# GpSimd makes the lower half of every second weight block of the up stage, from the eighth on

## The chip, the cores and the metric

One core of one Trainium2 chip runs the whole kernel. The metric is device time in microseconds (us). The engines have separate queues and meet only at semaphores: TensorE (PE) multiplies matrices, VectorE (DVE), ScalarE (ACT) and GpSimd (POOL) work elementwise, SyncE (SP) issues DMAs, and GpSimd issues the indirect ones (gathers of rows).

## What is computed

A decoder layer on 512 tokens of width 1024: a mixer, a cross-attention and a PEER channel mixer. Only the last matters here. Each token picks 16 of 16384 one-neuron experts for each of 8 heads and sums what they give:

```
u = jnp.take(expert_down, idx, axis=0)
a = jax.nn.gelu(jnp.einsum('nd,nhkd->nhk', xb, u).astype(jnp.float32), approximate=False)
w = (gb * a).astype(xb.dtype)
v = jnp.take(expert_up, idx, axis=0)
return jnp.einsum('nhk,nhkd->nd', w, v)
```

## The kernel before, in words

For three of the four tiles of 128 tokens (less 32 tokens) the kernel computes all experts densely: the down stage multiplies the activations with 128 blocks of 128 experts, and the **up stage** multiplies the gated result with the 128 blocks of `up_in` (128x1024 each, 512 KB). The fourth tile, the sparse one, gathers its rows of `up_in` one choice after the other: 128 gathers, each of which brings one row for each of the 128 tokens, and 128 weighted additions to `x`.

Float32 products are made of halves: a number is split into a rounded high part and a low part (the rest), and `three` adds high by high, high by low and low by high. So the up stage needs for every block `up_high` and `up_low` of the weights, and `wgt_high` and `wgt_low` of the gated activations.

The work on block u in the up stage, by engine:

- SP loads the block into one of eight places (`uraw`), when the product of block u-8 is done, and the gates and activations besides.
- ACT writes `up_high` (`high_up`, L585), as soon as the product of block u-4 is done, since there are four places for it; then `wgt_high` (L589).
- DVE goes through turns, one for each block (the loop at L1388 for blocks 0 to 14, the one at L1399 from 15 on). Turn u: `low_up(u)` makes `up_low` of block u (L1353, in the place of `uraw`), `weigh(u+1)` multiplies gates and activations of the next block (L1371, L1375), `weight_low(u)` makes `wgt_low` (L1382), and `sparse_up(u-1)` adds one gathered row to the sparse tile (L1361).
- POOL issues the 128 gathers in order (the loop at L528, L539). There are eight places for them; gather k waits for the addition of gather k-8 (`sparse_added`). Gathers 0 to 7 wait besides for the end of the down stage and for the first products, since their places are used before by other things.
- PE waits for `up_low` and `w_ready` of the block and then does 18 matmuls (`second_product`, L1776).

The order on each engine is written out by hand; no scheduler changes it. In the profile, `kept` and `arena` are the large buffers in which most of the named tensors lie.

Of the kernel before, what the change touches and what calls it, by code (L numbers as in the profile page):

```python
# [5 lines left out]
F32 = mybir.dt.float32  # L6
# [3 lines left out]
ALU = mybir.AluOpType  # L10
# [18 lines left out]
NK = 128  # L29
# [28 lines left out]
SLOTS = PH * TK  # L58
RING_A, RING_B, RING_C = 7, 4, 8
RING_U = 8  # L60
EDGE = 32
PARTS = P // EDGE
EDGE_SLOTS = SLOTS // PARTS
DE = DN - EDGE
E0, E_BASE = P - EDGE, P - 32
ROWS = SLOTS + EDGE_SLOTS
# [36 lines left out]
def build(nc, x_in, mem_in, vecs_in, final_in, ffn_in, front_w, keys_in, down_in, down_rows, up_in, out, gate_dram, hid_dram):  # L103
    ctx = ExitStack()
    with ctx:
        def sem(name):
            return ctx.enter_context(nc.semaphore(name))
# [4 lines left out]
        with ExitStack() as over:  # L112
            def aliased(name, kb, shape, now):
                if kb > now:
                    over.enter_context(nc.sbuf_tensor(f"pad{kb}", [P, (kb - now) * KB], F32))
                return over.enter_context(nc.sbuf_tensor(name, [P] + shape, F32R))
# [5 lines left out]
            up_hi = aliased("up_high", 140, [4, D], 133)  # L122
            memT_half = [aliased("memT_high", 188, [KC, NM], 156), aliased("memT_low", 196, [KC, NM], 196)]
            w_half = (w_hi, w_low)
        with ExitStack() as over:
            up_lo = aliased("up_low", 76, [RING_U, D], 0)
        with ExitStack() as over:
# [14 lines left out]
        def at(kb, n, *dims):  # L142

            where, kb = (kept, kb) if kb < 44 else (under_w, kb - 44) if kb < 60 else (arena, kb - 60)
            a = where[:, int(kb * KB):int(kb * KB) + n]
            if len(dims) == 2:
                return a.rearrange("p (a b) -> p a b", a=dims[0])
            if len(dims) == 3:
                return a.rearrange("p (a b c) -> p a b c", a=dims[0], b=dims[1])
            return a  # L150
# [91 lines left out]

        uraw = at(76, RING_U * D, RING_U, D)
        wraw = at(108, 4 * DN, 4, DN)
# [12 lines left out]
        ld_b = [sem(f"ld_down_rows_b{j}") for j in range(RING_B)]  # L257
        ld_c = [sem(f"ld_up_rows{j}") for j in range(RING_C)]
        dot_done, gel3_ready, sparse_added = sem("dot_done"), sem("gel3_ready"), sem("sparse_added")
        up_high, up_low = sem("up_high"), sem("up_low")  # L260
        consts = sem("consts")

        class Norm:
# [35 lines left out]
        stored = [sem(f"gates_stored{s}") for s in range(2)]  # L299
        ld_up = [sem(f"ld_up{s}") for s in range(RING_U)]  # L300
        ld_gate = [sem(f"ld_gate{s}") for s in range(4)]
# [27 lines left out]
        def up_slot(u):  # L329
            return (u + RING_U // 2) % RING_U  # L330

# [7 lines left out]
        def _(sp):  # L339
# [26 lines left out]
            def load_up(i, s):  # L366
                sp.dma_start(uraw[:, up_slot(s), :], up_in[bass.ds(i, 1)].rearrange("b p n -> (b p) n")).then_inc(ld_up[s], 16)

            def load_gates(i, s):

                sp.dma_start(gates[s], gate_dram[:, :, bass.ds(i * CH, GT * CH)]).then_inc(ld_gate[s], 16)
# [4 lines left out]
            def block_of(u):  # L376
                return u + SPILL if u < KEEP else u - KEEP
# [18 lines left out]
            load_gates(block_of(GT), 1)  # L396
            for u in range(5, RING_U):
                load_up(block_of(u), u)
            load_gates(block_of(2 * GT), 2)

            for s in range(2):
                sp.wait_ge(hid_stored[s], 16 * (SPILL // 2))
            for u in range(RING_U, KEEP):
                sp.wait_ge(up_done, u + 1 - RING_U)
# [34 lines left out]
        def _(pool):  # L439
# [57 lines left out]
            k = 0  # L497
# [27 lines left out]
            assert k == ROWS  # L525

            up_rows = up_in.rearrange("b p n -> (b p) n")
            for k in range(SLOTS):  # L528
                if k < RING:
                    pool.wait_ge(block_used, USED + NK - RING + k + 1)  # L530
                elif k == RING:
                    pool.wait_ge(block_used, USED + NK)
                if RING <= k < RING_C:
                    pool.wait_ge(up_done, k - RING + 1)
                if RING + 2 <= k < RING_C:
                    pool.wait_ge(w_raw, 2 * (3 if k == RING + 2 else 6))
                if k >= RING_C:
                    pool.wait_ge(sparse_added, k - RING_C + 1)
                nc.gpsimd.indirect_dma_start(rows_c[k % RING_C], None, up_rows,  # L539
                                             bass.IndirectOffsetOnAxis(idx3[:, k:k + 1].bitcast(U32), 0))\  # L540
                    .then_inc(ld_c[k % RING_C], 16)

        @block.scalar
        def _(act):
# [282 lines left out]
            def early_at(i):  # L827
                early(i, i % 4, 16 * ((USED + i + 2) // 4 + 1), USED + i + 1, 16 * (i // 2) if i > 1 else None, i + 3, i == 0)
# [9 lines left out]
            for q in range(PARTS):  # L838
                early_at(4 + q)
                act.dma_start(edge_h[q * EDGE:(q + 1) * EDGE], hn[E0:P, DT - 1, :].rearrange("p (k n) -> p k n", k=KC))\  # L840
                    .then_inc(edge_moved, 16)
# [9 lines left out]
            for n in range(DT):  # L851
# [3 lines left out]
                if n == 0:  # L855
                    early_at(EXP_AT[0])
                    for q in range(PARTS):
                        if q < 3:
                            early_at(EXP_AT[0] + 1 + q)
                        if q == 0:  # L860
                            act.wait_ge(idx_ready, 2)
                        act.dma_start(edge_idx[q * EDGE:(q + 1) * EDGE, :],
                                      idx_last[E0:P, q * EDGE_SLOTS:(q + 1) * EDGE_SLOTS]).then_inc(edge_moved, 16)
# [17 lines left out]
            for n in range(STEPS):  # L881
# [6 lines left out]
                if GEL_AT <= n < GEL_AT + PARTS:  # L888
                    q = n - GEL_AT
                    act.dma_start(edge_back[E0:P, q * EDGE_SLOTS:(q + 1) * EDGE_SLOTS],  # L890
                                  edge_gel[q * EDGE:(q + 1) * EDGE, :]).then_inc(edge_moved, 16)
                if n == LAST_TURN:
# [72 lines left out]
        def _(dve):  # L965
# [382 lines left out]
                nc.vector.memset(ones_of[:, :, DE:DN], 1.0).then_inc(edge_ones, 1)  # L1348


            def low_up(i, s):
                dve.wait_ge(up_high, i + 1)
                nc.vector.tensor_tensor(up_lo[:, up_slot(s), :], uraw[:, up_slot(s), :], up_hi[:, s % 4, :].bitcast(F32),  # L1353
                                        ALU.subtract).then_inc(up_low, 1)
# [9 lines left out]
            def weigh(i, s, quad, gate_landed, landed, block, kept_hid=None):  # L1364
                dve.wait_ge(ld_gate[quad], gate_landed)
                if kept_hid is None:
                    dve.wait_ge(ld_hid[s % 4], landed)
                else:
                    dve.wait_ge(gelu_out, landed)
                h = hidr[:, s % 4, :] if kept_hid is None else kept_hid  # L1370
                nc.vector.tensor_tensor(  # L1371
                    wraw[:, s % 4, 0:FAR * CH].rearrange("p (c n) -> p c n", n=CH),
                    h[:, 0:FAR * CH].rearrange("p (c n) -> p c n", n=CH),
                    gates[quad][:, :, (s % 4) * CH:(s % 4 + 1) * CH], ALU.mult).then_inc(w_raw, 1)
                nc.vector.tensor_tensor(  # L1375
                    wraw[:, s % 4, FAR * CH:].rearrange("p (i n) -> p i n", i=1),
                    h[:, FAR * CH:].rearrange("p (i n) -> p i n", i=1),
                    stage[:, FAR % 2, bass.ds(block, 1), :], ALU.mult).then_inc(w_raw, 1)

            def weight_low(i, s):  # L1380
                dve.wait_ge(w_high, i + 1)
                nc.vector.tensor_tensor(wgt_half[1][:, s, :], wraw[:, s, :], wgt_half[0][:, s, :].bitcast(F32),  # L1382
                                        ALU.subtract).then_inc(w_ready, 1)
# [2 lines left out]
            dve.wait_ge(edge_ones, len(hid_ones))  # L1386
            weigh(0, 0, 0, 16, SPILL + 3, SPILL, hid_kept[0])
            for s in range(15):  # L1388
                low_up(s, s % RING_U)
                weigh(s + 1, s + 1, (s + 1) // 4, 16, SPILL + s + 4, SPILL + s + 1, hid_kept[s + 1])  # L1390
                weight_low(s, s % 4)
                if s == 0:
                    dve.wait_ge(gel3_ready, 1)
                    step(nc.vector.tensor_tensor(w3, gel3, gate3, ALU.mult))
                else:
                    sparse_up(s - 1, (s - 1) % 8, 16 * ((s - 1) // 8 + 1), s - 1 if s > 1 else None)
# [40 lines left out]
        def _(pe):  # L1437
# [333 lines left out]
            def up_operands(o, s):  # L1771
                d = slice((o % 2) * 512, (o % 2 + 1) * 512)
                return ([w[:, s % 4, (o // 2) * P:(o // 2 + 1) * P] for w in wgt_half],
                        [up_hi[:, s % 4, d], up_lo[:, up_slot(s), d]])

            def second_product(i, s, first=False):  # L1776

                pe.wait_ge(up_low, i + 1)
                pe.wait_ge(w_ready, i + 1)
                for o in range(2 * DT):  # L1780
                    if first and o in (4, 5):
                        pe.wait_ge(gelu_out, NK + o - 3)
                    ins = three(psum[:, o, :], *up_operands(o, s), first, False)
                ins.then_inc(up_done, 1)
# [43 lines left out]
                second_product(s, s)  # L1828
            with pe.Fori(1, NK // RING_U - 1) as r:
                for s in range(RING_U):  # L1830
                    second_product(r * RING_U + s, s)
            for s in range(RING_U - 2):
                second_product(NK - RING_U + s, s)
            pe.wait_ge(up_low, NK)
            pe.wait_ge(w_ready, NK)
            for o in range(2 * DT):
                for s in (RING_U - 2, RING_U - 1):
# [50 lines left out]
```

## Time and profile before

| what | us |
|---|---|
| median of 3 runs | 1627.9 (1626.72 to 1633.07) |
| the profiled execution | 1624.01 |
| its span, first to last instruction | 1622.3 |
| up stage in it, first to last `up_low` subtraction | 1085.0 to 1600.7 |

All numbers of the trace are of this one execution, in us from the start of its span; the time outside the span is 1.7 us. A timeline row gives start, duration, engine, line, operation, output<-inputs with shapes, and in brackets how long the engine had been idle before it and what ended that. An instruction's duration overlaps with the next one's start by about 0.1 on DVE.

### The profile page before, as it was taken

What the parts mean: (1) busy time and instruction counts of PE and PEld (TensorE: products, weight loads), DVE (VectorE), ACT (ScalarE), POOL (GpSimd) and SP (SyncE); (2) the same over time, 40 slices, a digit from 0 to 9 for tenths busy, and PEclk for the clock granted to TensorE, in tenths of its full rate; (3) what the DMA queues carried; (4) which work ended last, traced back from release to release, by engine and by line L of the source; (5) the groups of instructions that cost most, each with busy time, mean ns of one, the idle gap of its engine ahead of it and who ended that gap; (6) DMA issues with size and microseconds to landing.
All of it is one profiled execution on the core that took longest, in us unless ns stands there. A gap on an engine that the chain in (4) does not pass through costs nothing.

```text
span 1622.3 us, 26556 instructions
## 1 busy us (share of the span) xinstructions
PE 1600.3 (99%) x9227; PEld 1422.6 (88%) x9227; DVE 1133.7 (70%) x2214; ACT 673.2 (41%) x998; POOL 829.1 (51%) x523
## 2 busy tenths in 40 slices
PE   8999999999999999999999999999999999999998
PEld 6888888788889999999999999998888888888886
DVE  4155451351509999996999898329888888888887
ACT  5342453451534343534545544444333333333333
POOL 4463276423244998987787777866422222222220
PEclk9999999999999999999999999999999999999999
DMA  4322242313434999997999999949999999999992
GB/s 184 93 100 71 75 151 94 104 53 117 146 102 131 347 340 332 329 335 233 339 405 394 387 403 401 362 158 391 400 348 350 331 349 339 349 334 348 339 331 77
DMA packets 154425, 424.69 MB, mean 262 GB/s; under 512 B 15728, under 2 KB 65904, under 8 KB 154224
## 3 DMA queue, kind: packets, MB, share of 16 engines
q1 hardware_dynamic: 89088, 229.41, 40.5%
q0 software_dynamic: 41472, 151.01, 25.5%
q10 hardware_dynamic: 23792, 43.33, 6.9%
q8 instruction: 42, 0.69, 0.2%
q14 instruction: 31, 0.25, 0.0%
HBM read 379.88 MB, written 43.25 MB: 261 GB/s over the span
## 4 chain that ended last, share of the span: by engine, by line
PE 69%; issue 16%; POOL 9%; DVE 2%; DMA 2%; ACT 1%; POOLq 0%; SPq 0%; ACTq 0%; DVEq 0%
PE psum L1471 22%; PE psum L1473 22%; PE psum L1472 22%; POOL w_low L461 8%; PE psum L1766 4%; DMA gate_dram<-arena 1%; DMA kept<-down_in 1%; POOL arena L493 1%; DMA arena<-down_rows,arena 0%; DVE arena L1258 0%; ACT w_high L581 0%; DVE arena L1202 0%; DVE arena L1193 0%; DVE arena L1194 0%; DMA kept<-front_w 0%
## 5 line engine op out<-in xcount | busy, mean ns | idle before, releaser
L461 POOL TENSOR_TENSOR w_low<-kept,w_high 128x1024 fp32r<-128x1024 f32 x212 | 519.5, 2454 | 320.3 <-ACT w_high L581 317.6
L1471 PE MATMUL psum<-hT_high,w_high 128*128 128x352 f32 (+2 forms) x1408 | 484.4, 344 | 7.2 <-POOL w_low L461 5.5
L1473 PE MATMUL psum<-hT_high,w_low 128*128 128x352 f32 (+2 forms) x1408 | 476.6, 339 | 0.0
L1472 PE MATMUL psum<-hT_low,w_high 128*128 128x352 f32 (+2 forms) x1408 | 476.4, 338 | 0.0
L581 ACT ACTIVATE w_high<-kept 128x1024 fp32r<-128x1024 f32 x212 | 224.0, 1058 | 202.6 <-DMA kept<-down_in 102.0
L1471 PE MATMUL psum<-up_high,wgt_high 128*128 128x512 f32 x768 | 298.8, 389 | 0.0
L1473 PE MATMUL psum<-up_high,wgt_low 128*128 128x512 f32 x768 | 298.8, 389 | 0.0
L1472 PE MATMUL psum<-up_low,wgt_high 128*128 128x512 f32 x768 | 298.8, 389 | 0.0
L1471 PEld LDWEIGHTS psum<-hT_high,w_high 128*128 128x128 f32 x1408 | 264.8, 188 | 24.2 <-POOL w_low L461 8.2
L1473 PEld LDWEIGHTS psum<-hT_high,w_low 128*128 128x128 f32 x1408 | 264.7, 188 | 12.7
L1472 PEld LDWEIGHTS psum<-hT_low,w_high 128*128 128x128 f32 x1408 | 264.8, 188 | 12.3 <-issue 0.5
L585 ACT ACTIVATE up_high<-arena 128x1024 fp32r<-128x1024 f32 x128 | 135.8, 1061 | 309.0 <-PE psum L1473 307.2
L1182 DVE CUSTOM_DVE_ANT_0 arena<-arena,psum 128x1024 f32<-128x1024 f32 x160 | 191.1, 1215 | 45.4 <-DMA arena<-down_rows,kept 42.6
L1353 DVE TENSOR_TENSOR up_low<-arena,up_high 128x1024 fp32r<-128x1024 f32 x128 | 156.9, 1226 | 76.4 <-ACT up_high L585 76.4
L1472 PEld LDWEIGHTS psum<-up_low,wgt_high 128*128 128x128 f32 x768 | 144.2, 188 | 29.9
L1471 PEld LDWEIGHTS psum<-up_high,wgt_high 128*128 128x128 f32 x768 | 144.2, 188 | 29.9
L1473 PEld LDWEIGHTS psum<-up_high,wgt_low 128*128 128x128 f32 x768 | 144.2, 188 | 29.8
L539 POOL DMA_INDIRECT arena<-up_in,kept x64 | 70.8, 1106 | 179.1 <-DVE kept L1361 166.4
L539 POOL DMA_INDIRECT kept<-up_in,kept x64 | 71.5, 1118 | 165.9 <-DVE kept L1361 157.7
L493 POOL DMA_INDIRECT arena<-down_rows,kept x128 | 121.8, 951 | 62.1 <-DVE kept L1182 30.4
L822 ACT ACTIVATE arena<-psum 128x352 f32<-128x352 f32 x112 | 51.9, 464 | 114.3 <-PE psum L1473 92.1
L1325 DVE TENSOR_TENSOR arena<-arena,psum 128x3072 bf16<-128x3072 bf16 x48 | 83.9, 1748 | 0.0
(252 smaller groups left out, 1956.4 us busy)
## 6 DMA issues: line engine op xcount, KB each, us to landing
kept<-down_in SPq DMA_DIRECT2D x128, 512.0 KB
arena<-up_in SPq DMA_DIRECT2D x128, 512.0 KB, 4.7
kept<-front_w SPq DMA_DIRECT2D x92, 512.0 KB
gate_dram<-arena ACTq DMA_DIRECT2D x40, 512.0 KB
hid_dram<-arena ACTq DMA_DIRECT2D x112, 176.0 KB
arena<-hid_dram SPq DMA_DIRECT2D x112, 176.0 KB
under_w<-gate_dram SPq DMA_DIRECT2D x24, 640.0 KB
arena<-gate_dram SPq DMA_DIRECT2D x8, 640.0 KB
```

The lines of the kernel that those rows point to most:

```text
L461: nc.gpsimd.tensor_tensor(w_low[:, s, :], ring[:, s, :], w_hi[:, s, :].bitcast(F32), ALU.subtract).then_inc(low_ready, 1)
L493: nc.gpsimd.indirect_dma_start(ring[slot], None, down_rows, bass.IndirectOffsetOnAxis((edge_idx if edge else idx3)[:, j:j + 1].bitcast(U32 ...
L539: nc.gpsimd.indirect_dma_start(rows_c[k % RING_C], None, up_rows, bass.IndirectOffsetOnAxis(idx3[:, k:k + 1].bitcast(U32), 0))\
L581: nc.scalar.activation(w_hi[:, s, :], ring[:, s, :], ACT.Copy).then_inc(high_ready, 1)
L585: nc.scalar.activation(up_hi[:, s % 4, :], uraw[:, up_slot(s), :], ACT.Copy).then_inc(up_high, 1)
L1182: nc.vector.tensor_tensor_reduce(ring[slot], ring[slot], h_row, 1.0, 0.0, ALU.mult, ALU.add, (edge_dot if edge else dot3)[:, j:j + 1]).the ...
L1325: nc.vector.tensor_tensor(hot_g[:, s], hot_i.rearrange("p (n q) i r -> p n q i r", q=1).to_broadcast(each), pieces[:, m:m + PAIRS].rearran ...
L1353: nc.vector.tensor_tensor(up_lo[:, up_slot(s), :], uraw[:, up_slot(s), :], up_hi[:, s % 4, :].bitcast(F32), ALU.subtract).then_inc(up_low, 1)
L1471: nc.tensor.matmul(out, lhs[0], rhs[0], start=first, stop=False)
L1472: nc.tensor.matmul(out, lhs[0], rhs[1], start=False, stop=False)
L1473: return nc.tensor.matmul(out, lhs[1], rhs[0], start=False, stop=last)
L1766: ins = nc.tensor.matmul(psum[:, (2 * h + m) % 3, t % 4 * P:(t % 4 + 1) * P], hot_j[:, h % HOTS, t // 2, :, t % 2], hot_g[:, h % HOTS, t / ...
```

## The change

From block 8 on, POOL makes `up_low` of the even blocks (60 of them, 8 to 126), DVE makes those of the odd blocks and of blocks 0 to 7. POOL does the subtraction of block u right behind its gather u+5, and the last two (124 and 126) behind gather 127. It signals on a semaphore of its own, `even_up_low`, on which PE waits for even blocks from 8 on. Nothing else is changed.

```diff
+POOL_UP = 8
...
+            def even_low_up(u):
+                s = u % RING_U
+                pool.wait_ge(up_high, u + 1)
+                nc.gpsimd.tensor_tensor(up_lo[:, up_slot(s), :], uraw[:, up_slot(s), :], up_hi[:, s % 4, :].bitcast(F32),
+                                        ALU.subtract).then_inc(even_up_low, 1)
+
             for k in range(SLOTS):
...
                 nc.gpsimd.indirect_dma_start(rows_c[k % RING_C], None, up_rows,
                                              bass.IndirectOffsetOnAxis(idx3[:, k:k + 1].bitcast(U32), 0))\
                     .then_inc(ld_c[k % RING_C], 16)
+                if k % 2 and k >= POOL_UP + 5:
+                    even_low_up(k - 5)
+            for u in range(SLOTS - 4, NK, 2):
+                even_low_up(u)
...
-            def low_up(i, s):
+            def low_up(i, s, late=True):
+                if late and s % 2 == 0:
+                    return
...
-                low_up(s, s % RING_U)
+                low_up(s, s % RING_U, s >= POOL_UP)
...
-            def second_product(i, s, first=False):
-
-                pe.wait_ge(up_low, i + 1)
+            def second_product(i, s, first=False, pairs=None):
+
+                if pairs is None:
+                    pe.wait_ge(up_low, i + 1)
+                elif s % 2:
+                    pe.wait_ge(up_low, pairs + (POOL_UP // 2 + (s + 1) // 2))
+                else:
+                    pe.wait_ge(even_up_low, pairs + (s // 2 + 1 - POOL_UP // 2))
```

POOL's queue at the start of the up stage, before. The first row is the last ten subtractions of the down stage, the others are the gathers 0 to 15, four to a row (by the buffer that they write):

```order
L461 TENSOR_TENSOR w_low<-kept,w_high 128x1024 x10
L539 DMA kept<-up_in,kept 128x1024 x4
L539 DMA arena<-up_in,kept 128x1024 x4
L539 DMA kept<-up_in,kept 128x1024 x4
L539 DMA arena<-up_in,kept 128x1024 x4
```

And with the change, up to gather 17:

```order
L462 TENSOR_TENSOR w_low<-kept,w_high 128x1024 x10
L546 DMA kept<-up_in,kept 128x1024 x4
L546 DMA arena<-up_in,kept 128x1024 x4
L546 DMA kept<-up_in,kept 128x1024 x4
L546 DMA arena<-up_in,kept 128x1024 x2
L532 TENSOR_TENSOR up_low<-arena,up_high 128x1024
L546 DMA arena<-up_in,kept 128x1024 x2
L532 TENSOR_TENSOR up_low<-arena,up_high 128x1024
L546 DMA kept<-up_in,kept 128x1024 x2
```

The subtraction of block 8 stands behind gathers 12 and 13, that of block 10 behind 14 and 15.

DVE's queue in turns 7 and 8, before, and the start of turn 9:

```order
L1353 TENSOR_TENSOR up_low<-arena,up_high 128x1024
L1371 TENSOR_TENSOR arena<-arena,under_w 128x320
L1375 TENSOR_TENSOR arena<-arena 128x64
L1382 TENSOR_TENSOR wgt_low<-arena,wgt_high 128x384
L1361 SCALAR_TENSOR_TENSOR kept<-arena,kept 128x1024
L1353 TENSOR_TENSOR up_low<-arena,up_high 128x1024
L1371 TENSOR_TENSOR arena<-arena,under_w 128x320
L1375 TENSOR_TENSOR arena<-arena 128x64
L1382 TENSOR_TENSOR wgt_low<-arena,wgt_high 128x384
L1361 SCALAR_TENSOR_TENSOR kept<-arena,kept 128x1024
L1353 TENSOR_TENSOR up_low<-arena,up_high 128x1024
```

And with the change (the lines are 13 further down):

```order
L1366 TENSOR_TENSOR up_low<-arena,up_high 128x1024
L1384 TENSOR_TENSOR arena<-arena,under_w 128x320
L1388 TENSOR_TENSOR arena<-arena 128x64
L1395 TENSOR_TENSOR wgt_low<-arena,wgt_high 128x384
L1374 SCALAR_TENSOR_TENSOR kept<-arena,kept 128x1024
L1384 TENSOR_TENSOR arena<-arena,under_w 128x320
L1388 TENSOR_TENSOR arena<-arena 128x64
L1395 TENSOR_TENSOR wgt_low<-arena,wgt_high 128x384
L1374 SCALAR_TENSOR_TENSOR kept<-arena,kept 128x1024
L1366 TENSOR_TENSOR up_low<-arena,up_high 128x1024
```

The subtraction has left turn 8; the other four instructions of the turn are the same.

## Rows read from the trace of the kernel before

**Rows 1.** The page, part 1: TensorE over the whole span.
```profile
PE 1600.3 (99%) x9227; PEld 1422.6 (88%) x9227; DVE 1133.7 (70%) x2214; ACT 673.2 (41%) x998; POOL 829.1 (51%) x523
```

**Rows 2.** Busy time in the up stage: PE, PEld, DVE, ACT, POOL, clock, DMA.
```profile
1093.00:1610.00 517.00, 517.00 (x2283) 428.32 (x2282) 435.56 (x634) 189.56 (x258) 139.53 (x126) 1.00 0.93 334
```

**Rows 3.** Waits from 1095 to 1602: engine, line, releaser, total, times, longest.
```profile
ACT up_high L585 <- PE psum L1473: 307.2, 120, 2.7
DVE up_low L1353 <- ACT up_high L585: 74.8, 115, 0.7
```

**Rows 4.** Timeline of one steady turn on ACT, DVE and POOL.
```profile
1154.87 1.06 ACT L585 ACTIVATE up_high<-arena 128x1024 fp32r<-128x1024 f32 x1 [2.61 <-PE psum L1473]
1155.96 1.23 DVE L1353 TENSOR_TENSOR up_low<-arena,up_high 128x1024 fp32r<-128x1024 f32 x1 [0.65 <-ACT up_high L585]
1157.64 0.55 DVE L1382 TENSOR_TENSOR wgt_low<-arena,wgt_high 128x384 fp32r<-128x384 f32 x1
1158.11 1.28 DVE L1361 SCALAR_TENSOR_TENSOR kept<-kept 128x1024 f32<-128x1024 f32 x1
1160.04 1.23 DVE L1353 TENSOR_TENSOR up_low<-arena,up_high 128x1024 fp32r<-128x1024 f32 x1 [0.65 <-ACT up_high L585]
...
1159.66 0.94 POOL L539 DMA_INDIRECT kept<-up_in,kept  x1 [3.14 <-DVE kept L1361]
```

**Rows 5.** Timeline of POOL in the down stage: subtraction, gather, subtraction.
```profile
899.14 2.40 POOL L461 TENSOR_TENSOR w_low<-kept,w_high 128x1024 fp32r<-128x1024 f32 x1 [0.81 <-ACT w_high L581]
901.69 0.95 POOL L493 DMA_INDIRECT arena<-down_rows,kept  x1
902.70 2.39 POOL L461 TENSOR_TENSOR w_low<-kept,w_high 128x1024 fp32r<-128x1024 f32 x1
```

**Rows 6.** Timelines: two places where POOL subtracts beside DVE.
```profile
104.75 3.63 POOL L461 TENSOR_TENSOR w_low<-kept,w_high 128x1024 fp32r<-128x1024 f32 x1 [7.20 <-ACT w_high L581]
...
106.04 2.39 DVE L1023 COPY kept<-arena 128x32 f32<-128x32 f32 x1
...
1086.62 2.82 POOL L461 TENSOR_TENSOR w_low<-kept,w_high 128x1024 fp32r<-128x1024 f32 x1 [4.55 <-ACT w_high L581]
...
1087.12 2.47 DVE L1394 TENSOR_TENSOR kept<-kept 128x128 f32<-128x128 f32 x1
```

**Rows 7.** Timeline of POOL: gathers 6, 8, 9, 10 and 13.
```profile
1106.14 1.88 POOL L539 DMA_INDIRECT arena<-up_in,kept  x1 [3.14 <-PE psum L1473]
...
1111.67 3.03 POOL L539 DMA_INDIRECT kept<-up_in,kept  x1 [0.30 <-issue]
1115.01 3.03 POOL L539 DMA_INDIRECT kept<-up_in,kept  x1 [0.30 <-issue]
1118.35 3.03 POOL L539 DMA_INDIRECT kept<-up_in,kept  x1 [0.30 <-issue]
...
1128.36 3.03 POOL L539 DMA_INDIRECT arena<-up_in,kept  x1 [0.30 <-issue]
```

**Rows 8.** Timeline of DVE: turn 5 in part, then turn 8 and the next start.
```profile
1106.12 0.49 DVE L1371 TENSOR_TENSOR arena<-arena,under_w 128x320 f32<-128x320 f32 x1
...
1118.34 1.23 DVE L1353 TENSOR_TENSOR up_low<-arena,up_high 128x1024 fp32r<-128x1024 f32 x1
1119.47 0.49 DVE L1371 TENSOR_TENSOR arena<-arena,under_w 128x320 f32<-128x320 f32 x1
1120.01 0.56 DVE L1382 TENSOR_TENSOR wgt_low<-arena,wgt_high 128x384 fp32r<-128x384 f32 x1
1120.47 1.29 DVE L1361 SCALAR_TENSOR_TENSOR kept<-arena,kept 128x1024 f32<-128x1024 f32 x1
1121.67 1.23 DVE L1353 TENSOR_TENSOR up_low<-arena,up_high 128x1024 fp32r<-128x1024 f32 x1
```

**Rows 9.** Timelines of PE and ACT where block 8's product begins.
```profile
1126.11 0.39 PE L1471 MATMUL psum<-up_high,wgt_high 128*128 128x512 f32 x1
...
1126.31 1.06 ACT L585 ACTIVATE up_high<-arena 128x1024 fp32r<-128x1024 f32 x1 [2.31 <-PE psum L1473]
```

More of the change, by code:

```diff
@@ L259, in build @@
         dot_done, gel3_ready, sparse_added = sem("dot_done"), sem("gel3_ready"), sem("sparse_added")
-        up_high, up_low = sem("up_high"), sem("up_low")
+        up_high, up_low, even_up_low = sem("up_high"), sem("up_low"), sem("even_up_low")
         consts = sem("consts")
@@ L1830, in _ @@
                 for s in range(RING_U):
-                    second_product(r * RING_U + s, s)
+                    second_product(r * RING_U + s, s, pairs=r * (RING_U // 2))
             for s in range(RING_U - 2):
-                second_product(NK - RING_U + s, s)
-            pe.wait_ge(up_low, NK)
+                second_product(NK - RING_U + s, s, pairs=(NK - RING_U) // 2)
+            pe.wait_ge(up_low, (NK + POOL_UP) // 2)
+            pe.wait_ge(even_up_low, (NK - POOL_UP) // 2)
             pe.wait_ge(w_ready, NK)
```

## The prediction

> **What bounds the kernel now.** I read the page first: TensorE is busy for 1600.3 of 1622.3 us [rows 1]. Then the busy time by stretches: in the up stage from 1093 to 1610 PE is busy for all of its 517 us, VectorE (DVE) for 435.6 and GpSimd (POOL) for 139.5 [rows 2]. The list of waits in the stage has no row in which PE waits at all; the longest is ScalarE (ACT), which waits 307.2 us for PE, and DVE waits 74.8 us for ACT, 115 times at most 0.7 [rows 3]. So PE sets the pace and the others follow it. One steady turn shows the distances [rows 4]: a turn is 1160.04 - 1155.96 = 4.08 us. ACT writes the high half of block u at 1154.87, when PE has ended block u-4; PE wants block u three turns later, at 1154.87 + 3 x 4.08 = 1167.1, and DVE has its last half ready at 1157.64 + 0.55 = 1158.2, 8.9 us early. A faster DVE can therefore give nothing here. The question is only whether POOL is ever late.
>
> **What goes.** 60 subtractions leave DVE, each 1.13 us from its start to that of the next instruction (1118.34 to 1119.47) [rows 8]. All of it lay beside PE: worth 0 on the path. What PE itself gets, one semaphore for another, I set at 0.
>
> **What comes, in the steady part.** POOL's subtraction of the same shape in the down stage takes 2.40 us, 0.06 behind a gather (901.69 + 0.95 to 902.70), and the next gather comes 0.15 behind it [rows 5]. It does not run freely beside DVE. A DVE instruction of 128x128 that met one took 2.47 us and a copy of 128x32 took 2.39 us [rows 6]: they stood until POOL was through. And POOL's own took 3.63 us where it met a long DVE instruction. They exclude each other, one whole instruction at a time. The Trainium skill says so (SBUF — State Buffer, "Who interferes with whom"): a DVE instruction with two SBUF inputs and a GpSimd instruction that reads SBUF take one shared read interface in turns, and the later one blocks fully; by that rule, too, every DVE instruction of a turn is exposed, and these rows agree.
>
> So DVE's load for two blocks is: a full turn back to back, 1121.67 - 1118.34 = 3.33; a turn without the subtraction, 3.33 - 1.13 = 2.20 [rows 8]; and up to 2.40 of standing still: 7.93 us, of 2 x 4.08 = 8.16. It still fits, by 0.23 us. Its place in the turn is kind: POOL may begin when ACT has written the high half, at 1154.87 + 1.06 = 1155.9, and is done at 1158.4; DVE's `wgt_low` then ends at 1158.9, where PE wants it at 1167.1. That leaves 8.2 us of cover. POOL's own load is 2.40 + 0.06 + 0.15 + two gathers of 0.94 with 0.30 between, 4.8 of 8.16 us, if the gathers stay at 0.94 [rows 4]. Queued behind the waiting subtraction are only the next gathers, with eight places, so that DVE wants a gather some seven turns after it can be issued. Cost of the steady part: 0.
>
> **What comes, at block 8.** Here the trace speaks against the change. The first subtraction is queued behind gather 13, and POOL is behind at that time: gather 8 starts at 1111.67, and it and the six behind it follow each other at 0.30 us with 3.03 us each, gather 13 from 1128.36 to 1131.39 [rows 7]. PE starts block 8 at 1126.11 [rows 9]. What it waits for would not even have been begun. A gather alone takes 0.94; it takes 3.03 where it begins with DVE's subtraction (1118.35 and 1118.34) and DVE then runs without a gap, and 1.88 where it begins with the next instruction (gather 6 at 1106.14, DVE's L1371 at 1106.12) [rows 7, 8]. Both ends lie 0.8 behind the end of DVE's L1382 (1120.01 + 0.56 = 1120.57, and the gather's 1121.38). The Trainium skill gives another rule (SBUF — State Buffer, the same section): a `tensor_tensor` is inferred not to hold up descriptor generation. By it the gathers would be short; the rows of 3.03 us beside nothing but such instructions say otherwise, and I go by the rows. What the rule would make of block 8 is the second rival.
>
> With the change DVE's turns 8 and 10 are short, so I lay the two queues side by side:
>
> - DVE: turn 8 starts at 1118.34 and takes 2.20, to 1120.54; turn 9 takes 3.33, to 1123.87; turn 10 takes 2.20, to 1126.07. Turn 11 has to wait for its high half, which ACT writes from 1126.31 to 1127.37 [rows 9]. So DVE is idle from about 1126.1 to 1127.4.
> - POOL: gather 10 at 1118.35 now begins with L1371: 1.88, to 1120.23. Gather 11 at 1120.53 begins with DVE's subtraction 9: 3.03, to 1123.56. Gather 12 at 1123.86 begins with L1371: 1.88, to 1125.74. Gather 13 at 1126.04 finds DVE idle: 0.94, to 1126.98. The subtraction of block 8 starts at 1127.04, ahead of DVE's at 1127.4, and takes 2.40, to 1129.44.
>
> PE could start at 1126.11 and starts at about 1129.5: **3.4 us of standstill**, which nothing gives back, since PE is full from there to the end. Bounds: at least 0, if the gathers 10 to 13 are 0.94 each (1118.35 + 4 x 1.24 + 2.40 = 1125.7, just in time); at most, gather 13 as before to 1131.39 and 2.46 more: 1133.85, which is 7.7 us, and up to 2.3 more if DVE's row of instructions is ahead of POOL at the port. I take 3.4, since its terms are the nearest rows.
>
> **Block 10 and on.** From 1129.5 every deadline is 3.4 us later: block 10 at 1129.5 + 8.16 = 1137.7. POOL has gathers 14 and 15 before it. From 1129.6, with DVE in a full turn 11, they take 1.9 to 3.0 and 0.94 to 1.9, then 0.6 of gaps and 2.40: done between 1135.4 and 1137.5. Just in time, with 0.2 to 2.3 us to spare; from then on POOL needs less than 8.16 for a pair and gains. Cost 0, upper bound about 2.
>
> **The sum.** 0 (DVE) + 0 (steady) + 3.4 (block 8) + 0 (block 10). The profiled execution of 1624.0 would become 1627.4; it lies 3.9 below the median, and the step is the same on it: 1627.9 + 3.4 = **1631.3 us**.
>
> **The rivals.**
>
> 1. *The gathers stay long, or block 10 stalls as well.* Gathers 8 to 14 are all 3.03 now, whatever else DVE does; for it: seven equal rows. Against: gather 6 with 1.88 and the idle gap that turn 11 gets. It gives 6 to 9 us: 1634 to 1637.
> 2. *POOL is in time.* If gathers 10 to 13 are 0.94 each, the standstill is 0, and the change is not seen at all: 1627.9. For it: the steady gather has 0.94 [rows 4]. Against: DVE has gaps in those turns, and not at block 8 until 1126.1.
> 3. *Slower by much: the pair does not fit.* A mechanism of the whole stage: with DVE at 7.93 of 8.16 us it has hardly gaps left, and the gathers may go back to 3.03 all along. Then POOL's pair is 2 x 3.03 + 0.30 + 0.06 + 0.15 + 2.40 = 8.97 us. It decides from 8.16 + 8.2 / 60 = 8.30 us on, where the cover is used up over the 60 pairs. At 8.97 the price is 60 x 0.81 - 8.2 = 40 us, or 1668; but each standstill of PE gives DVE gaps and shortens the gathers, so I expect 8.4 to 8.7 in this case: 6 to 24 us, 1637 to 1655. For it: the seven rows, just where DVE has no gap. Against: every pair has one turn in which DVE waits for ACT's high half, and one of the two gathers can fall there.
> 4. *It does not do what it says.* The queues show that DVE sheds one subtraction in two and POOL has it. Excluded, but for a side effect that I don't see.
>
> **How the numbers follow.** My forecast (2 to 5 us slower) 0.46; rival 1, 0.22; rival 2, 0.13; rival 3, 0.15; anything else, a gain among it, 0.04. About 0.5%, 8.1 us, is what a measurement of this kernel can tell from no change; so slower by more means over 1636.0: rival 3 and a fifth of rival 1, 0.19. A gain needs a PE wait that is not there: 0.02. The same: 0.79. The range goes from 1627 (rival 2, with the runs' lower half) to 1642, through rival 1 and the cheaper third of rival 3; above it lies about 0.1, below about 0.06.
>
> **What the changed profile would show.** Right: one wait of PE's first matmul of block 8 on POOL's `up_low`, 3 to 4 us, and no other wait of PE from there to 1610; POOL's first subtraction starting near 1127; gathers 10 and 12 below 2 us; steady POOL subtractions at 2.4 and a DVE instruction beside each with about 2 us more than before; DVE waiting for `up_high` once in two turns or less. Wrong: no PE wait (the gathers are not held up), a wait of 7 us and more (they are not shortened), or many PE waits spread to the end, with POOL never idle (rival 3).

## The result, and the profile after

| | median, us | before, measured beside it | ratio to before, 95% interval |
|---|---|---|---|
| changed | 1637.84 (1634.48 to 1639.96, 7 runs) | 1627.9 (1625.83 to 1633.36, 7 runs) | 1.0054 (1.0036 to 1.0073) |
| changed, measured again | 1636.0 (1631.24 to 1641.46, 6 runs) | 1627.18 (17 runs) | 1.0058 (1.0037 to 1.0078) |
| changed, a third time | 1632.73 (1628.02 to 1641.15, 10 runs) | 1627.02 (16 runs) | 1.0036 (1.002 to 1.0053) |

The change makes the kernel slower, by 6 to 10 us from median to median. The forecast was 3.4 slower, the range to 1642. The profiled execution took 1639.96 us, its span is 1638.2. Its line of the page that answers to [rows 1], and the two new or changed groups (line, engine, operation, count | busy us, mean ns | idle before, releaser):

```profile
PE 1605.0 (98%) x9227; PEld 1424.5 (87%) x9227; DVE 1173.1 (72%) x2154; ACT 671.6 (41%) x998; POOL 1016.0 (62%) x583
...
L532 POOL TENSOR_TENSOR up_low<-arena,up_high 128x1024 fp32r<-128x1024 f32 x60 | 144.2, 2404 | 128.8 <-ACT up_high L596 128.7
L1395 DVE TENSOR_TENSOR wgt_low<-arena,wgt_high 128x384 fp32r<-128x384 f32 x128 | 180.4, 1409 | 42.0 <-ACT wgt_high L600 42.0
```

POOL has 187 us more, as 60 subtractions at 2.4 us (144.2) and longer gathers make it: from 1150 to 1600 a gather takes 1.41 us in the mean (154.9 us for 110), where before it took 0.94. DVE did 60 instructions less and was yet *busier*, by 39 us: its L1395 (L1382 before, 0.55 us each [rows 4]) now has a mean of 1.41, since it stands still behind POOL.

The waits from 1085 to the end (who waited for whom: us in total, times, longest), where before PE had no row at all:

```profile
DVE wgt_low L1395 <- ACT wgt_high L600: 42.0, 58, 11.2
...
PE psum L1484 <- POOL up_low L532: 7.7, 1, 7.7
...
DVE arena L1384 <- DMA under_w<-gate_dram: 6.4, 1, 6.4
...
PE psum L1484 <- DVE wgt_low L1395: 1.6, 1, 1.6
```

There is one wait of PE on POOL's `up_low`, of 7.7 us, at block 8. The wait for `wgt_low` ends at 1110.7, before block 8, in turns that the change does not touch. The list has one more wait of PE, 0.4 us for the last subtraction of the down stage. Busy time by stretches (PE, PEld, DVE, ACT, POOL, granted clock, DMA share, GB/s), to be held against [rows 2]:

```profile
1093.00:1130.00 37.00, 35.44 (x163) 29.68 (x163) 28.66 (x44) 15.23 (x21) 21.49 (x12) 1.00 0.95 346
1130.00:1150.00 20.00, 12.32 (x42) 9.55 (x41) 8.85 (x13) 2.94 (x4) 16.82 (x10) 0.74 0.84 303
1150.00:1600.00 450.00, 450.00 (x1987) 372.60 (x1986) 418.80 (x498) 162.88 (x221) 286.48 (x165) 1.00 0.96 341
```

Apart from the 1.6 us ahead of 1130, all is lost in the 20 us around block 8; from 1150 to 1600 PE is busy all the time. And the middle row has a clock of 0.74. The place itself, POOL first (gathers 10, 11, 12, 13, then block 8's subtraction; compare [rows 7]), then DVE's subtraction of turn 11, then PE:

```profile
1125.00 1.90 POOL L546 DMA_INDIRECT kept<-up_in,kept  x1 [0.30 <-issue]
1127.21 3.03 POOL L546 DMA_INDIRECT kept<-up_in,kept  x1 [0.30 <-issue]
1130.55 1.90 POOL L546 DMA_INDIRECT arena<-up_in,kept  x1 [0.30 <-issue]
1132.75 3.03 POOL L546 DMA_INDIRECT arena<-up_in,kept  x1 [0.30 <-issue]
1135.80 3.10 POOL L532 TENSOR_TENSOR up_low<-arena,up_high 128x1024 fp32r<-128x1024 f32 x1
...
1132.74 1.22 DVE L1366 TENSOR_TENSOR up_low<-arena,up_high 128x1024 fp32r<-128x1024 f32 x1
...
1130.98 0.39 PE L1486 MATMUL psum<-up_high,wgt_low 128*128 128x512 f32 x1
1139.04 0.79 PE L1484 MATMUL psum<-up_high,wgt_high 128*128 128x512 f32 x1 [7.67 <-POOL up_low L532]
1139.63 0.63 PE L1485 MATMUL psum<-up_low,wgt_high 128*128 128x512 f32 x1
1140.05 0.63 PE L1486 MATMUL psum<-up_high,wgt_low 128*128 128x512 f32 x1
...
1145.45 0.39 PE L1484 MATMUL psum<-up_high,wgt_high 128*128 128x512 f32 x1
```

Gathers 10 to 12 took 1.90, 3.03, 1.90, as laid out. Gather 13 took 3.03. DVE was later, against PE, than in the trace of before: it had no gap at turn 11, and its subtraction started 0.01 us ahead of the gather. Then PE: its first matmul comes at 1139.04 where 1131.21 was due, 7.8 late. And the next ones follow at 0.42 to 0.43 us, not 0.23 [rows 9 has the place before]: 15 steps in 6.41 us, where 15 x 0.227 = 3.4 were due. The granted clock there is 0.50:

```profile
1139.00:1145.00 6.00, 5.96 (x14) 4.71 (x15) 0.00 (x0) 0.00 (x0) 5.22 (x4) 0.50 0.60 204
```

That is the lower of the two clock levels (1.2 GHz) behind a pause, and 3.0 us more.

Of the 15.9 us between the two profiled executions, 10.8 are this. The rest lies ahead of the first instruction that the change moves: the gates landed 3.3 us later for the first turn (1087.68 against 1084.41), and 1.6 are the wait for `wgt_low` ahead of block 8. That neither is an effect of the change is inferred from their place and not tested by itself.

### The profile page after: what moved, and what is told of

Same layout as the page of the kernel before. It is cut to its first block, busy times and chain, and to the rows that moved or that the text cites. A ratio compares the mean times of both kernels' runs of the same rounds, so it can differ in the third digit from the quotient of the medians.

```text
span 1638.2 us, 26542 instructions
## 1 busy us (share of the span) xinstructions
PE 1605.0 (98%) x9227; PEld 1424.5 (87%) x9227; DVE 1173.1 (72%) x2154; ACT 671.6 (41%) x998; POOL 1016.0 (62%) x583
## 4 chain that ended last, share of the span: by engine, by line
PE 62%; issue 16%; POOL 11%; DMA 5%; DVE 4%; ACT 1%; POOLq 0%; SPq 0%; DVEq 0%; ACTq 0%
PE psum L1484 20%; PE psum L1486 19%; PE psum L1485 19%; POOL w_low L462 9%; PE psum L1779 3%; DMA kept<-down_in 2%; POOL arena L494 1%; DMA under_w<-gate_dram 1%; DVE arena L1336 1%; DVE arena L1193 1%; DMA arena<-down_rows,kept 1%; POOL kept L546 1%; ACT w_high L592 1%; POOL arena L546 0%; DMA arena<-gate_dram 0%
## 5 line engine op out<-in xcount | busy, mean ns | idle before, releaser
L532 POOL TENSOR_TENSOR up_low<-arena,up_high 128x1024 fp32r<-128x1024 f32 x60 | 144.2, 2404 | 128.8 <-ACT up_high L596 128.7
L1395 DVE TENSOR_TENSOR wgt_low<-arena,wgt_high 128x384 fp32r<-128x384 f32 x128 | 180.4, 1409 | 42.0 <-ACT wgt_high L600 42.0
L546 POOL DMA_INDIRECT arena<-up_in,kept x64 | 90.8, 1418 | 36.9 <-DVE kept L1374 18.2
L546 POOL DMA_INDIRECT kept<-up_in,kept x64 | 94.7, 1480 | 27.0 <-DVE kept L1374 16.0
```

Source lines behind the costliest of these rows:

```text
L532: nc.gpsimd.tensor_tensor(up_lo[:, up_slot(s), :], uraw[:, up_slot(s), :], up_hi[:, s % 4, :].bitcast(F32), ALU.subtract).then_inc(even_up ...
```

## The experiments

**1. The change again, beside the others.** It was measured twice more, each time beside other kernels.

> The change once more, beside the three variants on the same chip. Theory (a standstill of TensorE at block 8 and a fall of its clock behind it): 8 to 12 us over the kernel before, one wait of 6 to 8 us on GpSimd's first subtraction, granted clock below 1 in the stretch behind it, no other wait on GpSimd. Rival (the steady load of the shared port costs as well): the same total, but with small waits spread to the end.

> The change once more, as the partner of the two others on the same chip: 7 to 11 us over the kernel before; a wait of TensorE of about 4.2 us where GpSimd's gather 13 takes 0.94 us, of about 7.7 us where it takes 3.03.

The medians were 1636.0 and 1632.73 us. The wait on POOL was 4.2 us in the first trace and 3.3 in the second, with no other wait on POOL's subtraction. The second trace, POOL's gathers 10 to 13 and the subtraction, and PE:

```profile
1120.30 1.90 POOL L546 DMA_INDIRECT kept<-up_in,kept  x1 [0.30 <-issue]
1122.50 3.03 POOL L546 DMA_INDIRECT kept<-up_in,kept  x1 [0.30 <-issue]
1125.84 1.89 POOL L546 DMA_INDIRECT arena<-up_in,kept  x1 [0.31 <-issue]
1128.04 0.94 POOL L546 DMA_INDIRECT arena<-up_in,kept  x1 [0.30 <-issue]
1129.00 2.36 POOL L532 TENSOR_TENSOR up_low<-arena,up_high 128x1024 fp32r<-128x1024 f32 x1
...
1131.49 0.79 PE L1484 MATMUL psum<-up_high,wgt_high 128*128 128x512 f32 x1 [3.33 <-POOL up_low L532]
1132.08 0.63 PE L1485 MATMUL psum<-up_low,wgt_high 128*128 128x512 f32 x1
...
1134.98 0.39 PE L1486 MATMUL psum<-up_high,wgt_low 128*128 128x512 f32 x1
```

This is the prediction's picture: 1.88, 3.03, 1.88, 0.94, then 2.40, and a wait of 3.4. Block 8 was due at 1128.0 and began 3.5 us late. Behind that come 1.7 us of slow matmuls (1131.49 to 1134.98 is 8 steps: 3.49, less 8 x 0.227), so 5.2 in all; in the first of the two traces it is 4.4 and 1.7, 6.1 in all. What differs between the executions is how long DVE waited for the first gates from DRAM (`under_w`) in turn 3. In the three traces of the change it waited 3.1, 4.0 and 6.4 us, and PE 3.3, 4.2 and 7.7. The two kernels of experiment 7, which have the same order on POOL, fit in: 3.2 and 5.4 us for the gates, and 3.4 and 5.0 from the time that PE was due at block 8 to the end of the subtraction.

The last step, from 5.0 to 7.7, is gather 13, and it hangs on very little. Here it is in the kernel with eight fillers of experiment 7, with DVE's subtraction of turn 11:

```profile
1131.19 0.94 POOL L546 DMA_INDIRECT arena<-up_in,kept  x1 [0.31 <-issue]
...
1131.21 1.23 DVE L1366 TENSOR_TENSOR up_low<-arena,up_high 128x1024 fp32r<-128x1024 f32 x1
```

DVE has no gap here either, but the gather began 0.02 us ahead of the subtraction, and took 0.94; in the profiled execution it began 0.01 behind it, and took 3.03.

The change's runs spread over 13 us (1628 to 1641) and those of before over 6 to 8. The wait for the gates would explain that, but runs without a trace cannot show it; what they do show is a lower granted clock in the slowest (0.996 at 1637.5 and 1641.2 us, 0.998 or 0.999 at 1628.0 and 1630.2).

**2. From block 16 on.**

```diff
-POOL_UP = 8
+POOL_UP = 16
...
-            for s in range(1, RING_U):
-                second_product(s, s)
-            with pe.Fori(1, NK // RING_U - 1) as r:
+            for s in range(1, POOL_UP):
+                second_product(s, s % RING_U)
+            with pe.Fori(POOL_UP // RING_U, NK // RING_U - 1) as r:
```

> GpSimd takes the even blocks from 16 on instead of from 8 on, 56 subtractions instead of 60; all else as in the change. Theory (all of the loss is the place of the first subtraction in GpSimd's queue, when it is behind): by block 16 the gathers have caught up, so no wait of TensorE on GpSimd; 0 us, within 0.15% of the kernel before; VectorE's instructions beside the subtractions still take about 2 us more. Rival (the exclusion of the two engines costs): 56 of 60 parts of the loss stay, 8 to 10 us slower than before.

1626.61 us, ratio 0.9999 (0.999 to 1.0008). PE has no wait on POOL, and its stretch is full again; DVE still stands beside each subtraction:

```profile
1093.00:1610.00 517.00, 517.00 (x2290) 428.96 (x2289) 478.67 (x580) 190.13 (x258) 329.74 (x185) 1.00 0.93 334
...
1299.83 2.44 DVE L1395 TENSOR_TENSOR wgt_low<-arena,wgt_high 128x384 fp32r<-128x384 f32 x1 [0.53 <-ACT wgt_high L600]
```

So 56 of the 60 subtractions cost nothing that these runs can tell (the interval ends 1.3 us above the kernel before). The loss needs a subtraction among the first four, at the place that they have in the queue.

**3. Earlier in the queue.**

```diff
-                if k % 2 and k >= POOL_UP + 5:
+                if k in (9, 11, 13, 15):
+                    even_low_up(k - 1)
+                if k % 2 and k >= 21:
                     even_low_up(k - 5)
```

> The same 60 subtractions as the change, from block 8 on, but those of blocks 8, 10, 12 and 14 stand behind gathers 9, 11, 13 and 15 (the change: 13, 15, 17 and 19), and the one of block 16 behind gather 21 as in the change. Theory (place in the queue): GpSimd's first subtraction starts near 1118 to 1122 in place of 1136, TensorE does not wait, 0 us against the kernel before, at most 0.15%. Rival (GpSimd or the port has too much to do at this time, wherever the subtraction stands): TensorE waits 3 us or more at block 8, 10 or 12, or the gathers come late and VectorE waits for them; 5 us or more slower.

1632.79 us, ratio 1.0036 (1.0022 to 1.0051): the expected 0 was missed, by 5.6 us. Block 8 and the next three have no wait. But block 16, which keeps its place behind gather 21, has one. POOL from block 14's subtraction to block 16's (the six gathers between take 1.3 to 3.0 us), and PE's wait:

```profile
1143.40 4.47 POOL L532 TENSOR_TENSOR up_low<-arena,up_high 128x1024 fp32r<-128x1024 f32 x1 [1.32 <-ACT up_high L598]
1148.03 1.76 POOL L546 DMA_INDIRECT kept<-up_in,kept  x1
...
1160.40 1.90 POOL L546 DMA_INDIRECT arena<-up_in,kept  x1 [0.30 <-issue]
1162.32 2.58 POOL L532 TENSOR_TENSOR up_low<-arena,up_high 128x1024 fp32r<-128x1024 f32 x1
...
1165.03 0.62 PE L1486 MATMUL psum<-up_high,wgt_high 128*128 128x512 f32 x1 [2.82 <-POOL up_low L532]
```

The standstill moved to the next subtraction that has six gathers ahead of it. DVE, stopped by the early subtractions, had no gap (it was busy for all 20 us from 1130 to 1150), and the gathers were long. Block 16 began 3.0 us late, and the slow matmuls behind the pause cost 1.7 more. I had not seen that when I chose block 16's place: the mistake of the change, made once more at another block.

**4. Fewer gathers ahead, throughout.** All 60 subtractions, the one of block u behind gather u+1 (lead 1, the edit below), or behind gather u+3 (lead 3).

```diff
-                if k % 2 and k >= POOL_UP + 5:
-                    even_low_up(k - 5)
-            for u in range(SLOTS - 4, NK, 2):
-                even_low_up(u)
+                if k % 2 and k >= POOL_UP + 1:
+                    even_low_up(k - 1)
```

> The same 60 subtractions; the one of block u stands behind gather u+1 throughout (the change: u+5). Theory: the first one starts near 1120 to 1123, there is never a row of several gathers ahead of one (as ahead of block 16 in the second variant), and TensorE does not wait: 0 us, within 0.15% of the kernel before. Rival (the next gathers now stand behind a subtraction that waits for ScalarE, and come too late): VectorE waits for gathers in every pair, and if that exceeds 8 us of cover TensorE waits for wgt_low; 5 us or more slower.

> The same 60 subtractions; the one of block u stands behind gather u+3. Theory (the wait grows with the number of gathers ahead): the first one starts behind gather 11, near 1130, and ends at 1132.5 to 1133.5, where TensorE wants it near 1130 to 1132: a wait of 0.5 to 2.5 us and about 1 us of slow matmuls, 1 to 3 us slower than before (ratio 1.0005 to 1.002), between the variant with lead 1 and the change. Rival (it depends on how busy the port is, not on the place): the same wait as in the change, 4 to 8 us.

Lead 1: 1627.34 us, ratio 0.9999 (0.999 to 1.0009). Lead 3: 1629.77, ratio 1.0024 (1.0009 to 1.0039), a bit more than the 1.002 expected. The first subtraction with lead 1, and with lead 3 together with PE's place:

```profile
1121.94 3.62 POOL L532 TENSOR_TENSOR up_low<-arena,up_high 128x1024 fp32r<-128x1024 f32 x1
```

```profile
1126.97 3.60 POOL L532 TENSOR_TENSOR up_low<-arena,up_high 128x1024 fp32r<-128x1024 f32 x1
...
1128.94 0.39 PE L1486 MATMUL psum<-up_high,wgt_low 128*128 128x512 f32 x1
1130.71 0.49 PE L1484 MATMUL psum<-up_high,wgt_high 128*128 128x512 f32 x1 [1.39 <-POOL up_low L532]
1131.04 0.40 PE L1485 MATMUL psum<-up_low,wgt_high 128*128 128x512 f32 x1
1131.28 0.39 PE L1486 MATMUL psum<-up_high,wgt_low 128*128 128x512 f32 x1
```

Lead 1, 3, 5: no wait, 1.4 us, 3.3 to 7.7 us. The same work, only its place is different. Note that the pause of 1.4 us leaves the clock alone: the matmuls behind it are back at 0.23. The traced execution of lead 3 (1628.7 us) lost 1.6 us at block 8; its 12 runs reach up to 1637.22. Where those lost more is not shown.

**5. The wait alone.** VectorE makes everything as before; TensorE only waits until GpSimd has come past gather 13.

```diff
                     .then_inc(ld_c[k % RING_C], 16)
+                if k == 13:
+                    nc.gpsimd.memset(at(23.25, 1), 0.0).then_inc(passed, 1)
...
             for s in range(1, RING_U):
                 second_product(s, s)
+            pe.wait_ge(passed, 1)
```

In its first form it had `pool.sem_inc(passed, 1)` in place of the memset:

> The kernel before, VectorE makes all lower halves; the only edit is that TensorE, ahead of block 8, also waits until GpSimd has issued gather 13, the place at which the change's first subtraction stands. Theory (the place in the queue does it, not the subtraction): the gathers 8 to 13 all take 3.03 us since VectorE has no gap, gather 13 ends some 5 us after TensorE wants block 8, and the clock falls behind it: 5 to 8 us slower (ratio 1.003 to 1.005). Rival (the subtraction itself or its contention makes the loss): a wait below 2 us, the time of the kernel before.

1627.11 us, ratio 1.0002 (0.9989 to 1.0015), and no wait of PE, though gather 13 ended at 1133.75 and PE started block 8 near 1128.5. The increment was not ordered behind the gathers' execution; this run says nothing about the theory. With the memset:

> The first form of this experiment measured nothing: the semaphore was raised by GpSimd's sequencer, which ran ahead of the gathers, so TensorE never waited. Now a memset of 128x1 on GpSimd stands behind gather 13 and raises it when it has run; TensorE waits for it ahead of block 8; VectorE makes all lower halves as before. Theory (the place in the queue makes the loss, with all gathers at 3.03 us): gather 13 ends 5 to 6 us after TensorE wants block 8, behind it some ten matmuls at the lower clock cost 2 us: 6 to 9 us slower than before, nearly all that the change loses. Rival (the subtraction and its contention make most of it): 0 to 3 us.

1635.57 us, ratio 1.0054 (1.004 to 1.0067), 8.6 us slower than before. Gather 13, the memset, and PE:

```profile
1128.02 3.04 POOL L540 DMA_INDIRECT arena<-up_in,kept  x1 [0.30 <-issue]
1131.05 0.12 POOL L544 MEMSET kept<- 128x1 f32 x1
...
1131.51 0.77 PE L1474 MATMUL psum<-up_high,wgt_high 128*128 128x512 f32 x1 [5.79 <-POOL kept L544]
```

A kernel in which POOL subtracts nothing in this stage loses as much as the change (5.7 us beside it, 8.8 and 9.9 in the other two measurements). So POOL's lateness at that point is enough for the loss; the kernel before has it, too, but nobody waited on it. In the change itself it is a part of the wait, since DVE's short turns shorten gathers 10 and 12. Gather 13 ended 1.0 us after PE was due in the third measurement's trace (1128.98 against 1128.01) and 4.6 us in the profiled one (1135.78 against 1131.21); the rest of the 3.5 and 7.8 us is the subtraction, 2.4 and 3.1 us, which costs nothing where its place is reached in time.

**6. All of it on GpSimd**, from block 16 on (112 subtractions). The edit also sets `POOL_UP` to 16 and makes PE wait for `even_up_low` at every block from there.

```diff
-                if k % 2 and k >= POOL_UP + 5:
+                if k >= POOL_UP + 5:
                     even_low_up(k - 5)
...
-                if late and s % 2 == 0:
+                if late:
                     return
```

> GpSimd makes the lower half of every block from 16 on (112 subtractions), VectorE none of them. Theory (the two engines exclude each other, so a subtraction on GpSimd costs VectorE 2.40 us in place of 1.13): two turns of VectorE are 2 x 2.20 + 2 x 2.40 = 9.2 us against 8.16 of TensorE; over 56 pairs that is 58 us, less the 8 us of cover: 40 to 55 us slower (ratio 1.025 to 1.034), TensorE waits on both halves to the end and VectorE has hardly an idle row. Rival (they run side by side, and what looks like standing still in the records is no real load): VectorE has 2 x 2.20 us of work, 0 us.

1697.01 us, ratio 1.0429 (1.0413 to 1.0445): 70.5 us slower, over the 40 to 55 expected. One turn on POOL, on DVE and the next on DVE, and the stretch:

```profile
1299.44 0.96 POOL L546 DMA_INDIRECT arena<-up_in,kept  x1 [1.36 <-DVE kept L1374]
1300.42 2.42 POOL L532 TENSOR_TENSOR up_low<-arena,up_high 128x1024 fp32r<-128x1024 f32 x1
...
1300.10 3.83 DVE L1374 SCALAR_TENSOR_TENSOR kept<-arena,kept 128x1024 f32<-128x1024 f32 x1
...
1304.86 3.83 DVE L1374 SCALAR_TENSOR_TENSOR kept<-arena,kept 128x1024 f32<-128x1024 f32 x1
...
1200.00:1600.00 400.00, 370.50 (x1525) 279.27 (x1524) 400.00 (x338) 125.26 (x170) 285.49 (x170) 1.00 0.86 293
```

DVE is busy for all 400 us, and bounds: a turn is 4.76 us. L1374 takes 3.83 in place of 1.28, so a subtraction on POOL costs DVE 2.55 us, more than its own 2.42. The DVE instruction starts 0.32 us ahead of the subtraction, beside the end of the gather, and ends 1.09 behind it; so most of those 0.32 us are lost as well. 112 x (4.76 - 4.08) = 76, less the 8.2 of cover, is 68 of the 70.5. PE waited only for `wgt_low` (94 times, 36.7 us in the list of waits), never for POOL's `up_low`; the expected wait on both halves was wrong.

**7. Busy while waiting.** Eight, and then five, plain matmuls between blocks 7 and 8, into an unused bank; nothing reads their results.

```diff
+            pe.wait_ge(ld_fin, 16)
+            for _ in range(8):
+                nc.tensor.matmul(psum[:, 7, :], ident, fin_w[:, 0:512], start=True, stop=True)
```

> The change, and TensorE runs eight plain float32 matmuls of 128x128 by 128x512 into an unused bank between blocks 7 and 8, in the time in which it would stand still (their results are not used). Theory (the pause costs twice: the wait, and then matmuls at the lower clock for some 15 instructions of 0.43 us instead of 0.23, 3.2 us): the granted clock stays 1.00, block 8's matmuls keep the distance of 0.23 us, and the kernel is 2 to 3.5 us faster than the change as sent again. Rival (the clock falls for another reason, or the slow matmuls are an effect of the wait itself): the matmuls behind the wait are slow all the same, and the time is that of the change or above it.

> The change with five plain float32 matmuls between blocks 7 and 8 in place of eight, 4.3 us in place of 6.9, which no longer reach past the end of the wait. Theory (the lower clock costs its own 1.6 to 3 us): the matmuls of block 8 keep 0.23 us, TensorE's rest of the wait is 0 to 3.5 us, and the kernel is 1.5 to 3 us faster than the change as sent in this call. Rival (the fillers do nothing for the time): within 0.5 us of the change.

Eight: 1635.13 us beside 1636.0 of the change. Five: 1634.71 beside 1632.73. Neither gained the 1.5 to 3.5 us expected. The traces show the part that I had right, eight fillers first, then five:

```profile
1129.64 7.03 PE L1849 MATMUL psum<-kept 128*128 128x512 f32 x16
1136.11 0.79 PE L1484 MATMUL psum<-up_high,wgt_high 128*128 128x512 f32 x1
1136.74 0.40 PE L1485 MATMUL psum<-up_low,wgt_high 128*128 128x512 f32 x1
1136.97 0.39 PE L1486 MATMUL psum<-up_high,wgt_low 128*128 128x512 f32 x1
```

```profile
1129.88 4.45 PE L1849 MATMUL psum<-kept 128*128 128x512 f32 x10
1133.77 0.80 PE L1484 MATMUL psum<-up_high,wgt_high 128*128 128x512 f32 x1
1134.40 0.40 PE L1485 MATMUL psum<-up_low,wgt_high 128*128 128x512 f32 x1
```

Behind fillers the matmuls keep 0.23 us: it is the idle pause that lowers the clock. But with eight fillers block 8 began 1.5 us after the end of the subtraction (1134.64), which ate the gain. With five, block 8 starts 3.9 us late and loses 0.4 more at its first step, 4.3 against 5.2 of the trace of the change shown in experiment 1: 0.9 us, below what runs that spread over 7 to 13 us can tell. The effect is shown in the rows and not in the time.

## Why the prediction was right, and where it was short

1. *PE bounds, and DVE's relief is worth nothing*: right. With the subtractions well placed the time is that of before to 0.1%. There was in fact no relief: from 1150 to 1600 DVE is busy for 418.8 us with the change and for 378.3 before.
2. *The engines exclude each other; the steady pair costs 0*: right, with wrong sizes, in both directions. In the steady part POOL begins in DVE's gap, where L1395 takes 2.44 in place of 0.55: 1.9 us and not 2.40, and the pair is 418.8 / 450 x 8.16 = 7.6 us. Where POOL's subtraction comes right behind a gather, it costs DVE 2.55 us (experiment 6), which would make the pair 5.53 + 2.55 = 8.08 of 8.16. The steady gathers did not stay at 0.94, on which the sum for POOL rested; with their mean of 1.41 its pair is 5.7 of 8.16 us, which still fits.
3. *POOL is late at block 8*: right in mechanism, place and sign. The durations 1.88, 3.03, 1.88 came true in every trace of the change; gather 13 was 0.94 in two and 3.03 in one. The wait was 3.3, 4.2 and 7.7 us; the forecast's 3.4 and its upper bound 7.7 are the two ends. The step that was mis-sized: I took DVE's distance from PE, and with it the gap of turn 11, from one trace. That distance goes with DVE's wait for the first gates, and that wait differs from run to run. With a longer wait POOL is later even where gather 13 stays at 0.94 (5.0 us with a wait of 5.4), and with no gap the gather is long or short by whether DVE's subtraction starts ahead of it.
4. *The sum was short by the clock*: I put the standstill at its own length. Behind the pauses of 2.8 to 7.7 us, 8 to 15 matmul steps run at 0.43 us: 1.7 to 3.0 us more, a third to a half on top. With it the best of the traces of the change is 5.2 and the worst 10.8, and the medians (6 to 10 over before) lie between. No row of the kernel before shows a pause in the up stage, but this term should have been in the bounds.
5. *Block 10 just in time*: right, no wait there. *Rival 3, the pair does not fit*: it did not happen. Experiment 6 overloads DVE and not POOL, whose gathers took 0.96 there, so it is not that rival's mechanism. (That rival's 1668 leaves out the 3.4 us of block 8, and its 1637 to 1655 has them.)
6. *The range held the time, in part by luck.* The medians lie 1 to 7 us above 1631.3, and none of them in the 2 to 5 us that had the highest chance. The range reached to 1642 for rivals 1 and 3, and neither happened: gathers 10 and 12 were short, block 10 had no wait, and none was spread over the stage. The line above which the kernel would be "slower" was 1636.0, with 0.19; of the three medians one is above it, one on it and one below. The profiled execution even shows a sign that was named as wrong, a wait of 7 us or more, but not for the reason given with it: two of the gathers 10 to 13 were shortened, and the wait was long all the same, since DVE and POOL ran later against PE.
7. *A reading of the rows* was not exact: the gathers of 3.03 us do not lie beside `tensor_tensor` instructions alone. Gather 10 ran from 1118.35 to 1121.38, and DVE's SCALAR_TENSOR_TENSOR at L1361 began at 1120.47. The long part lies beside the four instructions ahead of that, so the conclusion stands.

## What to carry to other kernels

Work that moves to an idle engine is placed in a queue: ask what stands ahead of it at the worst moment, here the start of a stage, not in the steady part. Six gathers of 3 us that nobody had waited for became the critical path by one semaphore, and moving the same work four places forward, or starting it eight blocks later, took the loss away, to 0.1%. A pause of the bounding engine has to be priced with the slow instructions behind it.

## What the runs showed of the hardware

- A gather's 0.94 us on GpSimd grows to 1.9 or 3.03 beside VectorE instructions with two SBUF inputs, depending on which it starts with; the same two figures came at gathers 8 to 12 in every trace of the change. In both cases it ends 0.8 us behind the last `tensor_tensor` of the turn, beside the SCALAR_TENSOR_TENSOR, which also reads two SBUF inputs. Other starts gave other lengths, such as 1.09 at 0.19 us ahead of L1374 (1297.02 and 1297.21) and 1.71 at 0.33 us behind L1366 (1298.75 and 1298.42), both in the profiled execution of the change. The Trainium skill (SBUF — State Buffer, "Who interferes with whom") infers that a `tensor_tensor` does not hold up descriptor generation; these rows disagree, and the kernel with lead 1 shows it again.
- The other way round, VectorE lost 2.55 us to a subtraction of 2.42 that followed a gather at once, in the steady turns of experiment 6. Around block 8 it was once 2.8: 3.00 in place of 0.22 for L1388, in the third measurement of the change.
- Out of a full stream of matmuls, TensorE's clock did not fall behind a pause of 1.4 us and fell behind those of 2.8, 3.3, 4.2, 5.8 and 7.7 us (the matmuls followed at 0.43 us). It did not fall where fillers ran in the pause.
- `sem_inc` on GpSimd, behind a gather in program order, was seen by TensorE over 5 us before that gather ended; a memset's increment was not.
